# A fused differential-attention layer: input projection as seven block products instead of eight, in two passes

## The reference, cut to what matters

```
mod = silu(c) @ ada_w[0] + ada_b[0];  shift, scale, gate = split(mod, 3)
h = rms_norm(x, norm_pre) * (1 + scale) + shift             # (1024, 2048)
q, k, v, z = h @ diff_w_in                                  # (2048, 8192), four slices of 2048
sc = q k^T * 128**-0.5, chunk-causal mask (chunks of 64), for 2 maps per head
p = softmax(sc);  attn = p[0] - lam * p[1];  o = attn @ v
o = rms_norm(o, subln) * (1 - lambda_init) * silu(z)
y = o @ diff_w_out                                          # (2048, 2048)
out = x + gate * rms_norm(y, norm_post)
```

## Time and profile before

| what | us |
|---|---|
| median of three runs | 2294.71 |
| lowest and highest of them | 2292.49, 2296.35 |
| span of the profiled execution | 2299.6 |
| TensorE busy in it | 2191.6 (95%) |
| VectorE busy | 858.5 (37%) |
| ScalarE busy | 580.0 (25%) |
| GpSimd busy | 190.7 (8%) |

### The profile page before, as it was taken

The page is one execution under the profiler, slowest core; times in us unless marked ns, Lnnn a source line. Parts: engine busy times, 40 slices in busy tenths (PEclk is TensorE's granted clock), DMA queues, the critical chain, the costliest instruction groups (busy, mean ns, idle before and its releaser), DMA issues.

```text
span 2299.6 us, 27998 instructions
## 1 busy us (share of the span) xinstructions
PE 2191.6 (95%) x10116; PEld 1777.6 (77%) x10116; DVE 858.5 (37%) x1472; ACT 580.0 (25%) x1167; POOL 190.7 (8%) x336
## 2 busy tenths in 40 slices
PE   2678999999999999999999999999999999999998
PEld 1567878888888778877887888788788877888876
DVE  5755632333233333322332233233323334444343
ACT  3233112222222222222222222222222223332241
POOL 2452000000000000000000000000000000000000
PEclk9779999999999999999999999999999999999999
DMA  9865734433443333434333333333334366445642
GB/s 304 261 221 175 263 107 131 128 108 103 121 123 110 102 119 115 115 101 141 115 106 113 121 115 106 111 119 115 106 109 127 105 200 217 151 149 198 211 155 73
DMA packets 393681, 325.96 MB, mean 142 GB/s; under 512 B 16998, under 2 KB 330444, under 8 KB 390860
## 3 DMA queue, kind: packets, MB, share of 16 engines
q1 hardware_dynamic: 393264, 324.09, 45.5%
q10 hardware_dynamic: 284, 0.05, 0.0%
HBM read 242.27 MB, written 81.80 MB: 141 GB/s over the span
## 4 chain that ended last, share of the span: by engine, by line
PE 91%; DVE 3%; SPq 1%; DMA 1%; issue 1%; POOL 1%; ACT 1%; DVEq 0%; POOLq 0%; ACTq 0%
PE ps L1217 29%; PE ps L1218 28%; PE ps L1219 28%; DVE acc L878 2%; PE ps L1291 1%; PE ps L1298 1%; PE ps L1201 1%; SPq L378 1%; PE ps L1314 1%; POOL hT_lo L581 1%; PE ps L1272 1%; DMA ada<-in_ada_w_dram 1%; DMA x_tok<-in_x_dram 0%; DMA q_sb<-q_dr 0%; PE ps L1212 0%
## 5 line engine op out<-in xcount | busy, mean ns | idle before, releaser
L1217 PE MATMUL ps<-hT_hi,w_hi 128*128 128x512 f32 x2048 | 840.6, 410 | 17.2 <-POOL hT_lo L581 17.2
L1218 PE MATMUL ps<-hT_lo,w_hi 128*128 128x512 f32 x2048 | 817.6, 399 | 0.0
L1219 PE MATMUL ps<-hT_hi,w_lo 128*128 128x512 f32 x2048 | 817.1, 399 | 0.0
L922 DVE TENSOR_TENSOR w_lo<-w_raw,w_hi 128x512 fp32r<-128x512 f32 x245 | 170.2, 695 | 1029.8 <-ACT w_hi L669 1029.8
L1217 PEld LDWEIGHTS ps<-hT_hi,w_hi 128*128 128x128 f32 x2048 | 390.7, 191 | 108.9 <-issue 18.5
L1219 PEld LDWEIGHTS ps<-hT_hi,w_lo 128*128 128x128 f32 x2048 | 389.9, 190 | 94.6
L1218 PEld LDWEIGHTS ps<-hT_lo,w_hi 128*128 128x128 f32 x2048 | 391.1, 191 | 83.2
L669 ACT ACTIVATE w_hi<-w_raw 128x512 fp32r<-128x512 f32 x245 | 154.1, 629 | 759.7 <-PE ps L1219 759.7
L1217 PE MATMUL ps<-w_hi,hT_hi 128*128 128x512 f32 x448 | 180.3, 403 | 0.0
L1219 PE MATMUL ps<-w_hi,hT_lo 128*128 128x512 f32 x448 | 177.9, 397 | 0.0
L1218 PE MATMUL ps<-w_lo,hT_hi 128*128 128x512 f32 x448 | 177.8, 397 | 0.0
(11 more groups left out here) (114 smaller groups left out, 1941.8 us busy)
## 6 DMA issues: line engine op xcount, KB each, us to landing
w_raw<-in_diff_w_in_dram SPq DMA_DIRECT2D x252, 256.0 KB, 2.9
ada<-in_ada_w_dram SPq DMA_DIRECT2D x64, 512.0 KB, 6.4
w_raw<-in_diff_w_out_dram SPq DMA_DIRECT2D x128, 256.0 KB, 3.1
ada<-in_ada_w_dram SPq DMA_DIRECT2D x16, 1024.0 KB, 7.2
q_dr<-ev SPq DMA_DIRECT2D x32, 512.0 KB
k_dr<-ev SPq DMA_DIRECT2D x32, 512.0 KB
v_dr<-ev SPq DMA_DIRECT2D x64, 256.0 KB
q_sb<-q_dr SPq DMA_DIRECT2D x64, 256.0 KB, 3.9
```

Of the source, the lines that this page charges most:

```text
L922: V.tensor_tensor(w_lo[:, j % 2], w_raw[:, j], w_hi[:, j % 2].bitcast(F32), ALU.subtract).then_inc(w_split, 1)
L1217: MM(dst, a_hi, b_hi, start=start, stop=False)
L1218: MM(dst, a_hi, b_lo, start=False, stop=False)
L1219: return MM(dst, a_lo, b_hi, start=False, stop=stop)
```

## The change

The four quarters of a head's projection (q, k, v, z: 256 features each) become groups of seven block products. The 256 features are two blocks of 128 and the 1024 tokens are two blocks of 512. The contraction is cut into even and odd k-tiles, and it is done in two passes: the first takes k-tiles 0 to 7, the second 8 to 15. In each pass a group is a 2x2x2 block product, done with seven products of sums instead of eight (224 products in each pass). One product has four k-tile pairs and three matmuls each: 12 matmuls of 512 columns.

- Pass one does all 32 groups, with no attention beside it. The results (four blocks of 128 x 512 per group) are stored to DRAM (d_dr) as partial sums. Beside it VectorE and TensorE make the second half of the mod sums and the gate, and h of k-tiles 8 to 15 is made, its sums of blocks too, and stored to DRAM (h_dr), from which pass two reads its seven blocks of 2 MB each.
- Pass two does the groups head by head, adds the partial sums that are loaded again, and writes q, k, v and z. The attention of head h-1 lies between the 28 products of head h, 3 per query block in blocks 0 to 3 and 4 in blocks 4 to 7.
- GpSimd makes four sums of weight blocks per group, VectorE four sums of activation blocks per pair of k-tiles.
- At the start, TensorE multiplies the first half of the shift and scale rows of ada_w by silu(c) itself: 32 steps of 8 matmuls with one moving column.
- All hardware loops are unrolled.

The order of work in pass two on the engines, from the diff:

```diff
+    SPREAD = [(1, 1, 1)] * 4 + [(1, 2, 1)] * 4
...
+            for h in range(1, HEADS):                       # SP
+                for qb in range(NB):
+                    n0, n1, n2 = SPREAD[qb]
+                    a = (h - 1) * NB + qb
+                    load_v(h - 1, qb)
+                    for _ in range(n0):
+                        slot(n)
+                        n += 1
+                    for _ in range(n1):
+                        slot(n)
+                        n += 1
+                    if a:
+                        store_oz(*before(a))
+                    load_qk(*divmod(a + 1, NB))
+                    for _ in range(n2):
+                        slot(n)
+                        n += 1
+                    load_z(h - 1, qb)
...
+                    if a:                                   # VectorE, after the n1 slots
+                        gate(*before(a))
+                    for i in range(n2):
+                        slot_w(n)
+                        if i == 0:
+                            aT_low(h - 1, qb)
+                        post_low(n - 2)
+                        n += 1
+                    if a:
+                        oz_low(*before(a))
...
+                    scores(h - 1, qb, 0)                    # TensorE
+                    for _ in range(n0):
+                        slot(n)
+                        n += 1
+                    scores(h - 1, qb, 1)
+                    for _ in range(n1):
+                        slot(n)
+                        n += 1
+                    if a:
+                        o_turn(*before(a))
+                    turn(h - 1, qb)
+                    for _ in range(n2):
+                        slot(n)
+                        n += 1
+                    weighted(h - 1, qb)
```

The product and the start of the mod sums:

```diff
+                for j in range(KB):
+                    last = three(ps[:, bank_of(i, pi)], ring[:, n % RING, 0, j], ring[:, n % RING, 1, j],
+                                 at_[:, 0, j], at_[:, 1, j], first and j == 0, j == KB - 1)
+                last.then_inc(prod, 1)
...
+            def ada_rows(s):
+                ch, r = divmod(s, 8)
...
+                pe.wait_ge(ada_in[s % 4], 32 * (s // 4 + 1))
...
+                for g in (2 * r, 2 * r + 1):
+                    for b in range(4):
+                        i = MM(ps[:, SC + b, 0:1], ada[:, s % 4, g % 2, b * P:(b + 1) * P], cact[:, g:g + 1],
+                               start=g == 0, stop=g == TG - 1)
+                i.then_inc(ada_used, 1)
...
+            def slot_w(n):                                  # VectorE
+                take(n - 1)
+                if n + LOOK < NALL:
+                    low_w(n + LOOK)
```

More of the change, by code:

```diff
@@ L48, in build @@
     AC = 512
[L49 to L52, removed]
     NB = SEQ // P
-    AHEAD = 4
+    LH = HEADS - 1
+    UK = 4
+    UNITS = KT // UK
+    KP = KT // 2
+    KB = KP // 2
+    PARTS_IN = 4
+    GP = PARTS_IN * HEADS
+    NP = 7
+    NA = GP * NP
+    NALL = 2 * NA
+    LOOK = 2
+    RING = 4
+    CCR = 5
+    P1, P2, P6, P5, P7, P3, P4 = range(NP)
+    C11, C12, C22, C21 = range(4)
+    BLOCK = {P2: C11, P7: C22, P3: C12, P4: C21}
+    ORDER = (C11, C22, C12, C21)
+    AT = {P2: 0, P7: 1, P3: 2, P4: 3}
+    SPREAD = [(1, 1, 1)] * 4 + [(1, 2, 1)] * 4
+    assert sum(map(sum, SPREAD)) == PARTS_IN * NP and len(SPREAD) == NB
+    PIECES = KP // 2
+    ADA0 = 4
+    MODS = 8
+    SCALE0 = 138
+    PREP0 = 148
+    PREP = 12
+    assert PREP0 + 4 * PREP < NA - 14
     GC = HALF
@@ L143, in build @@
[L143 to L155, removed]
@@ L289, in load_w @@
[L289 to L298, removed]
+                    sp.wait_ge(w_ok, NP * (i - 2) + P4 + 1)
+                k0, n0 = (i // GP) * KP, group_of(i) * 2 * P
@@ L464, in _ @@
+            for j in range(4):
+                load_wo(j)
+            load_oz_first(0, 1)
+            load_oz_first(0, 0)
+            load_oz_first(1, 1)
             load_oz_first(1, 0)
+            OZ_AT = {(0, 1): (2, 0), (0, 2): (2, 1), (1, 1): (3, 0), (1, 2): (3, 1)}
             u = 4
@@ L477, in _ @@
                         if qb == 0:
-                            for half in range(2):
-                                store(LH, COLS - 1, half)
+                            for pi in (P7, P3, P4):
+                                store(2 * GP - 1, pi)
                         if qb >= NB - UNITS:
@@ L483, in _ @@
                         if qb == 3:
-                            for half in range(2):
-                                sp.wait_ge(stored[half], HEADS * COLS * 32)
+                            sp.wait_ge(prod, NALL)
                             sp.wait_ge(gp_st, 16)
@@ new lines, in _ @@
+            for n in range(NA):
+                i, pi = divmod(n, NP)
+                if P6 <= pi <= P3:
+                    add_w(i + 1, pi - P6)
+                w, g = divmod(n - ADA0 - 16, 16)
+                if g == 0 and 0 <= w < MODS:
+                    pool.wait_ge(acc_ok, 16 * (w + 1))
+                    TTP(acc[:, w % 2, 0], acc[:, w % 2, 0], acc[:, w % 2, 1], ALU.add).then_inc(acc_sum, 1)
+                j, r = divmod(n - PREP0 - 4, PREP)
+                if 0 <= j < 4 and r < NP:
+                    low_blk(j * NP + r)
@@ L603, in _ @@
+            for qb in range(NB):
+                out_factor(LH * NB + qb)
             for n, tiles in enumerate([slice(0, HT)] + [slice(t, t + 1) for t in range(HT)]):
@@ new lines, in _, with post_high @@
+            for n in range(NA):
+                if n and (n - 1) % NP in (P1, P6, P5, P4):
+                    first_out(n - 1)
+                high_w(n + LOOK)
+                j, r = divmod(n - PREP0, PREP)
+                if 0 <= j < 4 and r < 4:
+                    modulate(16 + 4 * j + r)
+                if 0 <= j < 4 and 4 <= r < 4 + NP:
+                    high_blk(j * NP + r - 4)
+            def post_high(n):
+                if n < NA or n % NP not in BLOCK:
+                    return
+                i, pi = divmod(n, NP)
+                h, part = head_part(i)
+                b, o = BLOCK[pi], AT[pi]
+                e, x = o % 2, 4 * (i - GP) + o
+                if x >= 2:
+                    act.wait_ge(stored[e], 32 * (x // 2))
+                src = cc[:, buffer_of(i, b)]
+                if part == 2:
+                    act.wait_ge(vt_mm, 4 * h + o + 1)
+                    A(ev[:, e, 0], ps[:, VX], ACT.Copy).then_inc(post_hi, 1)
+                else:
+                    act.wait_ge(*read_out(i, pi))
+                    if part == 3:
+                        A(evf[:, e, 0], src, ACT.Tanh, scale=0.5).then_inc(post_hi, 1)
+                    else:
+                        A(ev[:, e, 0], src, ACT.Copy, scale=QKSCALE if part == 0 else 1.0).then_inc(post_hi, 1)
@@ L773, in y_square @@
             def y_square(G, t):
                 act.wait_ge(*bank_done(G, t))
-                if G == 0 and t == 0:
-                    for half in range(2):
-                        act.wait_ge(stored[half], HEADS * COLS * 32)
                 if G == GROUPS and t == 0:
@@ new lines, in post_low @@
+            def post_low(n):
+                if n < NA or n % NP not in BLOCK:
+                    return
+                i, pi = divmod(n, NP)
+                h, part = head_part(i)
+                b, o = BLOCK[pi], AT[pi]
+                e, src = o % 2, cc[:, buffer_of(i, b)]
+                if part == 1:
+                    return
+                dve.wait_ge(post_hi, 16 * h + 4 * part + o + 1)
+                if part == 0:
+                    i = STT(ev[:, e, 1], src, QKSCALE, ev[:, e, 0].bitcast(F32), ALU.mult, ALU.subtract)
+                elif part == 2:
+                    i = TTV(ev[:, e, 1], ps[:, VX], ev[:, e, 0].bitcast(F32), ALU.subtract)
+                else:
+                    i = STT(evf[:, e, 0], evf[:, e, 0], 1.0, src, ALU.add, ALU.mult)
+                i.then_inc(post_d, 1)
@@ L951, in maxes, with slot_w @@
+            def slot_w(n):
+                take(n - 1)
+                if n + LOOK < NALL:
+                    low_w(n + LOOK)
             def maxes(h, qb, m):
@@ L1062, in _, with before @@
-            for cc in range(COLS):
-                step(1, cc, cc > 0)
-            with dve.Fori(2, HEADS) as h:
-                for cc in range(COLS):
-                    step(h, cc, True)
-            LH = HEADS - 1
+                TTV(aT_lo[:, 0:qb + 1], ps[:, SC:SC + 2].rearrange("p b (n c) -> p (b n) c", c=P)[:, 0:qb + 1],
+                    aT_hi[:, 0:qb + 1].bitcast(F32), ALU.subtract).then_inc(at_done, 1)
+            def before(a):
+                return divmod(a - 1, NB)
+            for n in range(NA, NA + PARTS_IN * NP):
+                slot_w(n)
+                post_low(n - 2)
@@ new lines, in three @@
+            def three(dst, a_hi, a_lo, b_hi, b_lo, start, stop):
+                MM(dst, a_hi, b_hi, start=start, stop=False, skip_group_check=True)
```

(41 more changed lines are left out.)

1279 lines of the change are left out of this document (689 added, 590 removed).

## The result

The changed kernel takes 2453.44 us (median of 4 runs, 2443.29 to 2463.34) against 2295.53 us for the kernel before (median of 4): ratio 1.0677, 95% interval 1.0642 to 1.0713. It was forecast slower, 2532 us with a range from 2330 to 2640. Its profiled span is 2455.1 us.

A forecast was written before the change was run, and what follows sets the result against it. TensorE was taken as the bound from about 205 us on. Start 170, pass one 627 + 7 + 10, then 13 + 80, heads 841, stalls 242, clock 127, end 420 sum to 2537, so 2532 us; range 2330 to 2640.

The forecast's parts named there:

- first product starts: Start: loading x, then 32 ada_w steps on TensorE near the slow rate, put the first product at 170 us.
- pass one: 224 products of 2.8 us, 627 us, plus 7 for transposes and 10 for making the second half's blocks.
- between passes, head 0's products: Loading five 2 MB blocks between the passes leaves 13 us of waiting; head 0's 28 products then take 80 us.
- seven heads, unstalled: Pass two: seven heads of 120 us each without stalls, 841 us.
- pauses: Pass two: TensorE stalls for q and k about 4.4 us a query block, 55 times, 242 us; bounds 2 and 6.5.
- low clock in the heads: Pass two: matmuls behind each stall run at the lower clock, 2.3 us a block, 55 times, 127 us.
- end: After the heads: 412 us as before, plus 8 for output weights and oz loads issued later, 420 us.
- The mechanism: Pass two: oz_low comes late on VectorE and SP's store_oz waits for it ahead of load_qk, stalling TensorE in 55 blocks.
- the 1.79 us row: Old kernel's trace: after a 1.79 us TensorE pause no slower matmuls were seen, unlike after the 4.12 us pause.
- the row of 3.58 us per set: Start: eight one-column matmuls took 3.58 us after a pause, against 1.84 behind dense matmuls; forecast taken near the slow row.
- The 10 us for making the second half's blocks: Pass one: 28 parts through ScalarE, GpSimd and a 512 KB store were taken to cost 10 us, bounds 0 and 50.
- the rows of landing: Old trace's load landing times, 3.9 and 4.3 us, used for q and k in pass two: 5.65 us with SP's issues.

The follow-up runs named there:

- the first experiment: The changed kernel with SP issuing load_qk ahead of store_oz in pass two: 2157.92 us, ratio 0.9404 to the kernel before.
- the second experiment: The changed kernel with oz_low and oz_high put right behind gate, SP's order kept: 2295.01 us, ratio 0.9993 to the kernel before.
- third experiment: The changed kernel with the twelve matmuls of each query block's last product done twice (672 more): 2369.07 us, ratio 1.0317 to the kernel before.
- the fourth run: The changed kernel with load_qk ahead of store_oz and the last product's matmuls of each query block done twice: 2304.47 us, ratio 1.0045 to the kernel before.

## Why the prediction was right

| step | forecast us | measured us |
|---|---|---|
| first product starts | 170 | 163.2 |
| pass one | 644 | 629 (to 792.6) |
| between passes, head 0's products | 93 | 92 (to 884.8) |
| seven heads, unstalled | 841 | 831 (852.7 in the first experiment, less 22 of waits) |
| pauses | 242 | 210, of them 192 for q and k |
| low clock in the heads | 127 | 112 (1152.8 - 831 - 210) |
| end | 420 | 417 |
| sum | 2537 | 2455 |

Every term came out a little under its forecast: the 82 us between 2537 and 2455 are their sum, and no large error hides behind another. The unstalled heads are those of the first experiment, and the clock's 112 us is a remainder, checked below.

- The mechanism was read off the order of two lists, and it was right link by link. What was off is the size of the stall, 9.6 us from the last n1 product to k. In the block shown gate to scores took 8.3 us; q landed in 3.2 and k in 3.6 us (medians) where the earlier trace rows had 3.9 and 4.3. In the 6.6 us before that block's stores the DMA engines stood at a share of 0.00, so these loads found an empty queue; that this is why they landed sooner was not tried. It makes 3.5 us a pause for 4.4 forecast, within the bounds of 2 and 6.5.
- The clock term was priced at 2.3 us a block. A clock of 0.89 over 1152 us is some 250 us at the lower level. By the trace's clock records these are 52 falls for the 55 pauses, and TensorE stood still in 18 us of them; half of the rest is 116 us, 2.2 us a fall. So the remainder of 112 us is the clock, and price and count were both right.
- Shorter pauses do not each cost a little less. In the second and third experiment the pauses for q and k are 1.6 and 1.2 us on average (72 us in 45, 48 in 40). What is left above 831 us, the waits and the added matmuls (149, by the heads of the fourth run, 1001 us, against the first, 852) is 53 and 20 us. The clock records have 15 and 8 falls there (and in the second experiment the tail of an earlier one), worth 35 and 14 us; the other 18 and 6 us are not the clock, and no run says what they are. In the second experiment every fall stands behind a pause of 1.9 to 3.1 us, and no shorter pause has one. In the third all eight stand behind pauses of 1.33 to 1.92 us, while eight others of that length have none. So my reading of the 1.79 us row, that such a pause costs no clock, holds for some of them and not for all.
- The section "HAM oscillation — how this bites in real kernels" in the Trainium skill's "TensorE: Matmul & The Clock Gate", by which repeated waits for DMAs make every burst of matmuls start at the low clock, is borne out by the changed kernel (52 falls for 55 pauses). In the second experiment, with 15 falls for 45 pauses, not every burst starts low.
- Start: the row of 3.58 us per set was the right one to lean on; it ran at 3.45.
- Pass one was 15 us shorter. 2688 matmuls at 0.227 instead of 0.233 us are 16 of them. The 10 us for making the second half's blocks are not there: TensorE waited 1.5 us in all of pass one. In their place stand 6.5 us that the sum had left out, the 64 matmuls with one column (L1527) that sum the second half of the mod rows, and a remainder of about 4 us, with the first matmuls 0.43 us apart or more at the lower level. Inside this term, then, errors did cancel in part.
- What was removed is worth what was forecast: in pass one and in the unstalled heads the sum closes within 2.5%.
- The section "Anatomy of one DMA — SWDGE (gpsimd) path" in the Trainium skill's "DMA: Bandwidth & Descriptors" gives 3.8 us for oz, q and k together, as an estimate from its fit for another issue path. From the first oz store to the scores took 5.0 us in the block shown; the rows of landing, with 5.65, were nearer and a little high. The prediction's "about 50 us less" by that estimate does not follow from its own terms: 5.65 less 3.8, 55 times, is 102 us.

Open: whether the second 128 KB oz store in front of q delays its landing; it was not tried alone.

## What to carry to other kernels

When work is cut into smaller pieces between two dependent steps, list for every in-order queue what now stands in front of the next step's loads, and where the instruction that it waits for has gone: one store that waits for a late, unhurried result can cost more than the matmuls that were saved. Price a repeated TensorE pause with the slow matmuls behind it. And try the cheapest edit first, the order of two DMAs.

## What the runs showed of the hardware

- TensorE can be busy for 110 us with hardly a gap and stay at its low clock level nearly all the time: with one-column fp32 matmuls (108.2 of 110 us busy, granted 0.52), and even with one 384-column fp32 matmul among each eight of them (108.8 us, 0.52). With 512-column fp32 matmuls in their place the granted clock was 0.92.
- A window's granted clock reads 1.00 until the first change is recorded: the changed kernel's start shows 0.98 in 60 to 120 us with steps of 3.45 us, the first experiment 0.53 over the same stretch with the same steps. The first clock record of the one trace lies 114 us into the span, that of the other 37 us. The spacing of the matmuls is the safer sign.
- Shorter pauses made the granted clock fall more seldom, not less far: 52 falls for 55 pauses of 3.5 us on average, 15 for 45 of 1.6 us, 8 for 40 of 1.2 us, and some 2 us lost by each fall.
- The products' 512-column fp32r matmuls start 0.227 us apart, the old units' 0.233. Nothing here says why.

```profile
300.63 0.39 PE L1478 MATMUL ps<-blk,ring 128*128 128x512 f32 x1
300.86 0.39 PE L1479 MATMUL ps<-blk,ring 128*128 128x512 f32 x1
301.09 0.39 PE L1477 MATMUL ps<-blk,ring 128*128 128x512 f32 x1
```
